# Retention heads of a hybrid decoder step: samples one chunk behind the prompt, another order of keys, loads and output drains

## What is computed

```python
def retention_chunk(state, q, k, v, log_decay):
    ...
    inter = jnp.einsum('bhcd,bhde->bhce', q, state) * q_decay[None, :, :, None]
    scores = jnp.einsum('bhid,bhjd->bhij', q, k) * dmask[None]
    o = inter + jnp.einsum('bhij,bhje->bhie', scores, v)
    new_state = state * jnp.exp(C * log_decay)[None, :, None, None] + \
        jnp.einsum('bhjd,bhje->bhde', k * k_decay[None, :, :, None], v)
    return o, new_state
```

## Time and profile before

| what | value |
|---|---|
| time, median of 3 runs | 3241.62 us (3238.12 to 3246.32) |
| the profiled execution | 3239.39 us, its span 3237.7 us |
| granted TensorE clock, mean | 0.986 |
| busy: TensorE matmuls, DVE, ACT, POOL | 96%, 50%, 27%, 6% |
| retention heads in the span | from 2062 to about 2480 us |
| load or store of one sample's state, 512 KB, issue to landing | 5.2 us median, stores 7.6 us at most |
| cut of a weight unit, high part on ACT, low part on DVE | 1.91 us, 2.30 us mean |
| one `y_low` in the chunk loop | 0.97 us |

### The profile page before, as it was taken

The page is one execution under the profiler, slowest core; times in us unless marked ns, Lnnn a source line. Parts: engine busy times, 40 slices in busy tenths (PEclk is TensorE's granted clock), DMA queues, the critical chain, the costliest instruction groups (busy, mean ns, idle before and its releaser), DMA issues.

```text
span 3237.7 us, 50261 instructions
## 1 busy us (share of the span) xinstructions
PE 3112.0 (96%) x19898; PEld 2897.3 (89%) x19898; DVE 1620.1 (50%) x3140; ACT 859.4 (27%) x2161; POOL 194.4 (6%) x270
## 2 busy tenths in 40 slices
PE   7999989879999999999999999899999999999999
PEld 6877778749999999999798998788789999999999
DVE  7464738767444454447231222355656445444453
ACT  6342436604111111113222121433534111111110
POOL 0000001003000000002000000011113000000000
PEclk9999999979999999999999999999999999999999
DMA  6222256476211111111313222566561111111111
GB/s 225 90 92 101 70 178 181 132 256 257 85 52 39 39 47 57 52 39 40 109 58 128 81 97 100 182 201 225 178 226 66 40 39 65 48 43 39 39 39 52
DMA packets 152561, 330.83 MB, mean 102 GB/s; under 512 B 18400, under 2 KB 71808, under 8 KB 136376
## 3 DMA queue, kind: packets, MB, share of 16 engines
q1 hardware_dynamic: 134728, 200.23, 18.4%
q0 software_dynamic: 17712, 128.98, 11.2%
HBM read 255.19 MB, written 101.76 MB: 110 GB/s over the span
## 4 chain that ended last, share of the span: by engine, by line
PE 86%; DVE 4%; DMA 3%; issue 3%; ACT 2%; SPq 1%; POOL 1%; DVEq 0%; ACTq 0%; POOLq 0%
PE ps L993 61%; PE ps L1011 18%; PE ps L1110 1%; DMA ret_s<-zS 1%; DMA zV<-v_rows 1%; PE ps L1275 1%; PE ps L1006 1%; PE ps L1094 1%; PE ps L1280 1%; ACT sc L781 1%; DVE sc L1424 1%; DVE al L1435 1%; ACT wH L697 0%; POOL acc L397 0%; DVE wL L1333 0%
## 5 line engine op out<-in xcount | busy, mean ns | idle before, releaser
L993 PE MATMUL ps<-hH,wH 128*128 128x344 f32 x2880 | 921.0, 320 | 0.8 <-DVE hL L1339 0.8
L993 PE MATMUL ps<-hH,wL 128*128 128x344 f32 x2880 | 919.0, 319 | 0.0
L993 PE MATMUL ps<-hL,wH 128*128 128x344 f32 x2880 | 918.3, 319 | 0.0
L993 PEld LDWEIGHTS ps<-hH,wH 128*128 128x128 f32 x2880 | 541.8, 188 | 2.5 <-issue 0.9
L993 PEld LDWEIGHTS ps<-hH,wL 128*128 128x128 f32 x2880 | 541.0, 188 | 0.0
L993 PEld LDWEIGHTS ps<-hL,wH 128*128 128x128 f32 x2880 | 539.9, 187 | 0.7
L1333 DVE TENSOR_TENSOR wL<-raw,wH 128x2048 fp32r<-128x2048 f32 x123 | 283.0, 2301 | 360.5 <-ACT wH L697 360.2
L697 ACT ACTIVATE wH<-raw 128x2048 fp32r<-128x2048 f32 x122 | 231.0, 1910 | 747.6 <-PE ps L993 660.6
L1011 PE MATMUL ps<-wH,hH 128*128 128x512 f32 x832 | 332.6, 400 | 24.5 <-DVE hL L1339 18.2
L993 PE MATMUL ps<-hidH,wH 128*128 128x344 f32 x1056 | 339.1, 321 | 0.0
L993 PE MATMUL ps<-hidH,wL 128*128 128x344 f32 x1056 | 338.2, 320 | 0.0
(11 more groups left out here) (186 smaller groups left out, 3714.0 us busy)
## 6 DMA issues: line engine op xcount, KB each, us to landing
raw<-in_w POOLq DMA_DIRECT2D x123, 1024.0 KB, 5.2
qkv_rows<-ot SPq DMA_DIRECT2D x72, 256.0 KB, 2.0
zS<-in_state_in SPq DMA_DIRECT2D x32, 512.0 KB, 5.2
ret_s<-zS SPq DMA_DIRECT2D x32, 512.0 KB, 5.2
kv_s<-in_cache SPq DMA_DIRECT2D x2, 8160.0 KB
qkv<-qkv_rows SPq DMA_DIRECT2D x48, 256.0 KB, 4.1
g_cols<-rw SPq DMA_DIRECT2D x48, 172.0 KB, 2.4
v_rows<-rw SPq DMA_DIRECT2D x32, 256.0 KB, 2.1
```

What stands on the lines that cost most here:

```text
L993: mm = pe.matmul(out, lhs[k][a], rhs[k][b], start=(k == 0 and q == 0), stop=(k == n - 1 and q == 2))
```

## The change

On TensorE the 16 matmuls of a sample run one chunk later, in chunks 1 to 7 and once behind chunk 7. On ACT the first `z_scale` leaves the head's start: samples 0 and 1 are scaled in chunk 1 (ahead of the root, and behind the squares), sample `ch` in chunk `ch` ahead of the root. On DVE sample 0 is updated in chunk 1, samples 1 and 2 in chunk 2, and sample `ch` in its chunk from there; in chunks 0 and 1 the turn of the next queries comes directly behind the mask. SP issues chunk 1 ahead of sample 0 and each next chunk ahead of the sample before it; in head 0 `eye` and `gsel` follow sample 0. At the head's end ACT cuts unit `U_RO+2` ahead of the sample's root, DVE drains jobs 0 to 3 ahead of the sample's reciprocal, cuts the unit and drains job 4 ahead of the sample's product, and TensorE takes the product with `gsel` ahead of job 2 and the turn of `zo` ahead of job 5. Nothing that is computed changes.

```diff
--- before.py
+++ after.py
@@ -640,12 +640,17 @@
                 sp.dma_start(zV[:, k, :], v_dram[head, b:b + 1, :].rearrange("a t n -> (a t n)").partition_broadcast(P))\
                     .then_inc(z_loaded[k], 16)
 
-            def chunk_loads(h):
+            def chunk_loads(h, first=False):
                 head = bass.ds(h, 1)
+                chunk_load(h, 1)
                 z_load(h, 0)
-                for n in range(1, RS):
+                if first:
+                    sp.dma_start(eye[:, :, :, :], c["eye"]).then_inc(table_loaded, 16)
+                    sp.dma_start(gsel[:, :], c["gsel"]).then_inc(table_loaded, 16)
+                for n in range(2, RS):
                     chunk_load(h, n)
-                    z_load(h, n)
+                    z_load(h, n - 1)
+                z_load(h, RS - 1)
                 for b in range(NS):
                     sp.wait_ge(z_new, h * (2 * NS) + (2 * b + 2))
                     sp.sem_inc(sp_gate, 1)
@@ -668,9 +673,7 @@
             for b in range(RW):
                 sp.wait_ge(rstored[b], 16 * (RH * r_stores_to(27, b) + 1))
             sp.wait_ge(job_done, J_RO)
-            sp.dma_start(eye[:, :, :, :], c["eye"]).then_inc(table_loaded, 16)
-            sp.dma_start(gsel[:, :], c["gsel"]).then_inc(table_loaded, 16)
-            chunk_loads(0)
+            chunk_loads(0, True)
             with sp.Fori(1, RH) as h:
                 head_load(h)
                 chunk_loads(h)
@@ -915,7 +918,6 @@
                     act.wait_ge(rsum_done, h * 8 + (ch + 1))
                     act.activation(rr[:, ch % 2, :], ps[:, 6, 0:P], ACT.Sqrt, bias=epsb, scale=1.0 / RV).then_inc(rroot_ready, 1)
 
-                z_scale(0)
                 for ch in range(8):
                     k = ch % 2
                     act.wait_ge(k_up, h * 8 + (ch + 1))
@@ -923,28 +925,31 @@
                                    scale=kdec[ch]).then_inc(kd_ready, 1)
                     if ch >= 2:
                         y_cut(ch - 2)
+                        z_scale(ch)
+                    if ch == 1:
+                        z_scale(0)
                     if ch:
                         y_root(ch - 1)
-                    if ch + 1 < NS:
-                        z_scale(ch + 1)
                     act.wait_ge(up_done, h * 8 + (ch + 1))
                     if ch == 0:
                         act.wait_ge(state_stored, h * 16 + 16)
                     act.activation(state[:, :, :], ps[:, 2:4, :], ACT.Copy, scale=grow[ch]).then_inc(st_ready, 2)
                     act.wait_ge(ro_done, h * 8 + (ch + 1))
                     act.activation(rsq[:, :, :], ps[:, 4 + k, :].rearrange("p (e t) -> p e t", e=4), ACT.Square).then_inc(rsq_ready, 1)
+                    if ch == 1:
+                        z_scale(1)
                 y_cut(6)
                 y_root(7)
                 act.wait_ge(z_read, h * NS + (NS + RS))
                 act.activation(zo[:, :], ps[:, 7, 0:P], ACT.Square, accum_out=zl[:, 0:1]).then_inc(zl_step, 1)
                 y_cut(7)
+                cut_hi(U_RO + 2, J_RO, h, 3, RO_J)
                 act.wait_ge(zl_summed, h + 1)
                 act.activation(zl[:, 1:2], ps[:, 6, P:P + 1], ACT.Sqrt, bias=epsb, scale=1.0 / RV).then_inc(zl_step, 1)
                 act.wait_ge(zr_ready, h + 1)
                 act.activation(zo[:, :], ps[:, 7, 0:P], ACT.Copy, scale=zl[:, 2:3]).then_inc(zo_ready, 1)
                 act.wait_ge(zy_step, h + 1)
                 act.activation(yH[:, :, 0:NS], zy[:, :, :], ACT.Copy).then_inc(zy_hi, 1)
-                cut_hi(U_RO + 2, J_RO, h, 3, RO_J)
                 if not last:
                     cut_hi(U_RO + 3, J_RO + 2 * KC + 3, h, 3, RO_J)
                     cut_hi(U_RO + 4, J_RO + 2 * KC + 6, h, 3, RO_J)
@@ -1262,6 +1267,17 @@
                         pe.wait_ge(rroot_ready, h * 8 + ch)
                     pe.matmul(ps[:, 6, 0:P], ones[:, :], rsq[:, 0, :], start=True, stop=True).then_inc(rsum_done, 1)
 
+                def samples(b):
+                    if b == 0:
+                        pe.wait_ge(zm_ready, h * 2 + 2)
+                        pe.wait_ge(zo_ready, h + 1)
+                    pe.wait_ge(z_new, h * (2 * NS) + (2 * b + 2))
+                    for f in range(2):
+                        for j in range(4):
+                            mm = pe.matmul(ps[32 * j:32 * j + 32, 7, 0:P], zm[:, f, b, :], zS[:, b % RS, f, j * P:(j + 1) * P],
+                                           start=(b == 0 and f == 0), stop=(b == NS - 1 and f == 1))
+                    mm.then_inc(z_read, 1)
+
                 keys(0)
                 for ch in range(8):
                     k = ch % 2
@@ -1286,27 +1302,23 @@
                     mm.then_inc(ro_done, 1)
                     if ch < 7:
                         keys(ch + 1)
-                    if ch == 0:
-                        pe.wait_ge(zm_ready, h * 2 + 2)
-                        pe.wait_ge(zo_ready, h + 1)
-                    pe.wait_ge(z_new, h * (2 * NS) + (2 * ch + 2))
-                    for f in range(2):
-                        for j in range(4):
-                            mm = pe.matmul(ps[32 * j:32 * j + 32, 7, 0:P], zm[:, f, ch, :], zS[:, ch % RS, f, j * P:(j + 1) * P],
-                                           start=(ch == 0 and f == 0), stop=(ch == NS - 1 and f == 1))
-                    mm.then_inc(z_read, 1)
+                    if ch:
+                        samples(ch - 1)
+                samples(NS - 1)
 
                 def before(n):
                     if n == 0:
                         pe.wait_ge(y_lo, h * 8 + (6 + RS))
                     if n == 1:
                         y_sum(7)
+                    if n == 2:
+                        pe.wait_ge(st_ready, h * 16 + 16)
                         pe.wait_ge(zl_step, h * 2 + 1)
                         pe.wait_ge(table_loaded, 16 * 10)
                         pe.matmul(ps[:, 6, P:P + 1], gsel[:, :], zl[:, 0:1], start=True, stop=True).then_inc(zl_summed, 1)
-                    if n == 2:
-                        pe.wait_ge(st_ready, h * 16 + 16)
                     if n == 4:
+                        pe.wait_ge(y_ready, h * 8 + 7)
+                    if n == 5:
                         pe.wait_ge(y_lo, h * 8 + (8 + RS))
                         pe.wait_ge(zo_ready, h + 2)
                         pe.sem_inc(pe_gate, 1)
@@ -1706,11 +1718,19 @@
                     dve.wait_ge(r_loaded[ch % RS], h * (64 * 8 // RS) + 64 * (ch // RS + 1))
                     tt(qd[:, ch % 2, :, :], rqT[:, chunk_slot(ch), :, :], qdec[:, :].rearrange("p (a t) -> p a t", a=1).broadcast_to([P, 2, P]), ALU.mult).then_inc(qd_ready, 1)
 
+                def z_add(b):
+                    dve.wait_ge(z_scaled, h * NS + (b + 1))
+                    for f in range(2):
+                        stt(out=zS[:, b % RS, f, :], in0=zV[:, b % RS, :], scalar=zq[:, 1, f, b:b + 1], in1=zS[:, b % RS, f, :],
+                            op0=ALU.mult, op1=ALU.add).then_inc(z_new, 1)
+
                 turn(0)
                 for ch in range(8):
                     k = ch % 2
                     dve.wait_ge(rs_done, h * 8 + (ch + 1))
                     tt(sT[:, k, :], ps[:, 1, 0:P], dmask[:, :], ALU.mult).then_inc(sT_ready, 1)
+                    if ch < 2:
+                        turn(ch + 1)
                     if ch == 0:
                         dve.wait_ge(zqg_loaded, h * 48 + 48)
                         dve.wait_ge(table_loaded, 16 * 10)
@@ -1719,28 +1739,31 @@
                                 mm = tt(zm[:, f, :, r * NS:(r + 1) * NS], zq[:, 0, f, :].rearrange("p (a b) -> p b a", a=1).broadcast_to([P, NS, NS]),
                                         eye[:, :, r, :], ALU.mult)
                             mm.then_inc(zm_ready, 1)
+                    if ch == 1:
+                        z_add(0)
                     if ch >= 2:
                         y_low(ch - 2)
-
-                    dve.wait_ge(z_scaled, h * NS + (ch + 1))
-                    for f in range(2):
-                        stt(out=zS[:, ch % RS, f, :], in0=zV[:, ch % RS, :], scalar=zq[:, 1, f, ch:ch + 1], in1=zS[:, ch % RS, f, :],
-                            op0=ALU.mult, op1=ALU.add).then_inc(z_new, 1)
-                    if ch < 7:
-                        turn(ch + 1)
+                        if ch == 2:
+                            z_add(1)
+                        z_add(ch)
+                        if ch < 7:
+                            turn(ch + 1)
                     if ch:
                         y_rest(ch - 1)
                 y_low(6)
                 y_rest(7)
                 y_low(7)
+                for n in range(4):
+                    out_drain(J_RO, n, h, RO_J)
                 dve.wait_ge(zl_step, h * 2 + 2)
                 dve.reciprocal(zl[:, 2:3], zl[:, 1:2]).then_inc(zr_ready, 1)
+                cut_lo(U_RO + 2, h, 3)
+                out_drain(J_RO, 4, h, RO_J)
                 dve.wait_ge(zo_turned, h + 1)
```

(3 more changed lines are left out.)

## The result

The changed kernel takes 3217.4 us (median of 6 runs, 3214.3 to 3218.8) against 3241.1 before (6 runs, 3238.1 to 3246.3). The ratio is 0.9925 with a 95% interval of 0.9912 to 0.9938, so 23.7 us less. I had said 3225, and 3217 to 3219 for the rival in which the clock holds.

What follows compares the result with a forecast made beforehand. TensorE is busy 96% of the span, so only idle time and slow clock can be won: 41.7 us gone minus 25.0 new, net 16.7, giving 3222.7, or 3225 as median. Own range 3220 to 3230; with rivals 3214 to 3236.

Steps and rivals of the forecast that it cites:

- the rival in which the clock holds: Chunk 3 of each head: TensorE waits, but its clock does not fall; 3217 to 3219 us, chance 0.24.
- the first rival: The jam in chunk 3 without the fall of the clock: 6.4 us and up to 1.4 more saved, chance 0.24.
- What goes, 41.7 us: All savings in the retention heads: 33.4 us of waits, 0.7 for POOL, 4.8 for clock drops, 2.8 low-clock stretch.
- The 33.4 us: TensorE's waits within reach in the four retention heads, such as 9.6 us at head 0's start and 13.8 for state copies.
- The 4.8 us for three falls of the clock: Chunk loops of heads 0, 1, 3: three clock drops after waits of 1.97 to 2.39 us, about 1.6 us each, go.
- Part 1: Head 0's start: TensorE waits 1.8 us instead of 9.6; new 3.7 for chunk 1, 2.0 low clock, 1.5 in chunk 2.
- Part 2: Chunks 0 and 1 of every head: first sample's 1.1 us wait goes; new 0.35 us wait for POOL's sums, 1.4 in four.
- Part 3: Chunk 2's doubled updates jam: L1275 of chunk 3 waits 2.05 us per head, 8.2 us, plus four clock drops, 6.4 us.
- The four falls of the clock: One clock drop behind the chunk 3 wait in each of four heads, 6.4 us in sum.
- a border between 1.73 and 1.97 us: TensorE's chunk loops: the clock held after a 1.73 us idle gap and fell after 1.97; a drop costs about 1.6 us.
- Part 4: Later chunks: sample loads keep 1.9 and 1.8 us of room, so 13.8 us of state-copy waits go, and 0.5 for `ry`.
- Part 5: Head's end: 5.5 us before job 6, 2.9 for the square and 0.7 for POOL go; `zo` has 0.6 us room.

Runs made afterwards that it cites:

- e1: The kernel before with the new order at a head's end alone; 3229.2 us, ratio 0.9968 to before.
- e5: The changed kernel with DVE's update of sample 1 in chunk 2 ahead of `y_low(0)` instead of behind it; 3217.2 us, ratio 0.9926 to before.
- e4: The changed kernel with one more DVE addition of 128x512 in chunk 2 of each head, into an unused tile; 3220.4 us, ratio 0.9937 to before.
- e2: The changed kernel with the old order at a head's end; 3226.9 us, ratio 0.9955 to before.

## Why the prediction was right, and where it was off

The time was inside the range and the direction right, but the forecast's own mechanism did not come about. 3217.4 lies below its own range of 3220 to 3230, and heads 1 to 3 are those of the first rival, which had a chance of 0.24: a jam, and no fall of the clock. Of the sum, point by point:

**What goes, 41.7 us.** The 33.4 us of the earlier trace rows went, but for the 1.8 us ahead of the first state matmuls, which the sum had put back itself. The 4.8 us for three falls of the clock were real in the profiled execution, but e1 shows that they are not a property of those gaps: it has the same waits without a fall.

**Part 1, head 0.** 1.8 us and the landing at +9.0 were right (1.76 and +9.3), and the keys start 0.01 us behind the end of the table load (2068.48), so no drain of 1.38 us stands there. One step that failed is the sentence that nothing of TensorE waits for `zm` before the end of chunk 1. The mask of chunk 1 stands behind `zm` on DVE, and cost 1.45 us; the first sample cost 0.92 more, where head 0 of before had no such wait. I followed `zm` to its reader and not to what is queued behind it. The other is that chunk 0 was to run at full clock and the low stretch to follow the wait for chunk 1. It ran at the low clock after 1.76 us of idle time, 2.8 us longer than in head 1 (from L1296 to L1291 6.2 us without the wait, against 3.4), and the wait for chunk 1 shrank to 1.16 us: 4.0 us together where the sum had 3.7 + 2.0. The wait in chunk 2 came out at 1.65 us where the sum had 1.5 for sample 2, but on another path: ahead of `turn(2)` DVE waited 0.90 us for the load of chunk 2, until 2082.64, and worked without a pause from there to the `ry` that L1291 waits for. That term was right by luck.

**Part 2.** The 1.4 us for POOL's sums were too many. The second addition took 0.45 us, not 0.79, and ended at 2178.73, just when L1291 did:

```profile
2178.79 0.49 PE L1268 MATMUL ps<-rsq,ones 128*128 128x128 f32 x2
```

That is 2.00 us behind the start of L1291, against 1.89 in the next chunk. L1291 of chunks 1 and 2 stand 6.26 and 6.27 us apart in heads 1 and 2 and 6.02 in head 3, with 6.05 for an undisturbed chunk: 0.4 us in all.

**Part 3, the jam.** Right in place and cause (e5), the size 1.58 instead of 2.05. The next instruction of DVE follows the start of `y_low(0)` by 0.61 us (2184.64 to 2185.25), not by 0.97, and the keys and `y_cut(0)` end 0.88 us after `z_scale(1)` instead of 1.0. The four falls of the clock, 6.4 us, were the largest error, and it is one of method. I took a border between 1.73 and 1.97 us from four gaps of one execution. In the changed kernel's heads the gaps are 1.5 to 1.6 us, below that border, so the trace alone could leave the rule alive; e4 and e1 are what kills it.

**Part 4.** No wait for the state copy is left. The chunk loads take 2.3 us that the sum had not: it had looked at the samples' loads only, while `turn(7)` waits for the load of the chunk. Its room of 1.9 and 1.8 us was also counted behind a jam of 2.05 us and a fall of the clock; with 1.58 us and no fall, TensorE is at chunk 7 about 2 us sooner. The 3.2 us for 512 KB that the prediction set beside the measured 5.2 is the fit of the Trainium skill ("DMA: Bandwidth & Descriptors", Anatomy of one DMA) for DMAs that GpSimd issues, while SP issues these; in the changed kernel their medians are 5.0 us (load) and 5.5 us (store).

**Part 5.** The listed waits of 8.4 us are exact (e2), and what they are worth is 10.4 us, where the sum had 9.1 with the wait for POOL. `zo` was ready 0.7 us ahead of its turn; I had said 0.6.

Together, by three stretches of the traces, what the sum had gained and what was measured:

| stretch | sum, us | measured, us |
|---|---|---|
| head 0's first transposes to its chunk 1 | 4.9 | 7.2 |
| chunks 1 to 7 of the four heads | 1.6 | 6.1 |
| chunk 7 to the next head's chunk 1, or to the end | 10.2 | 12.5 |
| all | 16.7 | 25.9 |

The middle row is mostly the four falls that did not come and the shorter jam, less the waits for the mask and the first sample in head 0 and those of chunk 7. In the last, 1.3 of the 2.3 us are what a wait costs beyond its listed idle time; the other 1.0 I can't place. The rows did not cancel each other: all three came out better than the sum.

## What to carry to other kernels

When a step is moved on an in-order engine, follow what stands behind it in that queue as well as who reads it: the late tables cost 1.45 us through a mask that has nothing to do with them. A shift by one stage turns several small waits into one jam where the stages overlap, and when the jam is thinned out the next limit (here the transfers) takes the gain: 0.5 us won in chunk 3 of each head came back in chunks 6 and 7. The idle times in the list of waits gave less than the waits cost (8.4 of 10.4 us at the heads' ends); the distance between the same two blocks, compared across kernels, gives the whole. A rule on the clock drawn from a handful of gaps in one execution is no term for a sum; take it as a rival with a chance.

## What the hardware showed beside that

The same DVE subtraction of 128x512 (`y_low`) takes 0.69 us in one place and 0.98 in another of the same head loop. Each time it takes 0.97 or 0.98 in the changed kernel's heads, POOL's second addition starts just ahead of it and runs beside it (2299.18 and 2299.22 above); where it takes 0.69 in chunk 2 (2184.64), POOL is idle. POOL's addition takes 0.46 us alone (2183.58) and the same beside `y_low`, but 0.79 beside DVE's update. The Trainium skill ("SBUF — State Buffer", SBUF: two separate sides) says that a port pair shared by the two is locked for a whole instruction where DVE has two SBUF inputs, and that the loser blocks. The trace agrees in kind and not in size: DVE came second and took 0.29 us more, less than the 0.42 for which the addition still ran. No run here took POOL's additions away, so this is read from the traces and not tested.
